# First block of a two-block transformer: the projection of queries, keys and values and the attention as one stage, head by head

## What is computed

```python
def project(h):
    q, k, v = jnp.split(h @ w_qkv, [A_WIDTH, 2 * A_WIDTH], axis=-1)
    q = rms_gain(q.reshape(B, -1, A_HEADS, 2, A_HEAD_DIM), q_gain)
    k = rms_gain(k.reshape(B, -1, A_HEADS, 2, A_HEAD_DIM), k_gain)
    return q, k, v.reshape(B, -1, A_HEADS, A_V_DIM)
q_l, k_l = apply_rope(q_l, rc, rs), apply_rope(k_l, rc, rs)   # latent tokens only
def attend(q, k, v):
    s = jnp.einsum('bqhcd,bkhcd->bhcqk', q, k).astype(jnp.float32) * scale
    p = jax.nn.softmax(s, axis=-1)
    a = (p[:, :, 0] - lam * p[:, :, 1]).astype(v.dtype)
    return jnp.einsum('bhqk,bkhe->bqhe', a, v)
def finish(o):
    o = rms_gain(o, subln_gain) * (1.0 - lam_init)
    return o.reshape(o.shape[0], o.shape[1], A_WIDTH) @ w_o
```

## Time and profile before

| | |
|---|---|
| median of three runs | 3884.35 us |
| the profiled execution, its time | 3887.47 us |
| its span in the profile | 3885.7 us |
| TensorE matmul busy | 3619.6 us, 93% of the span |
| TensorE weight load busy | 3133.7 us, 81% |
| VectorE, ScalarE, GpSimd busy | 2536.4, 1596.2 and 697.0 us |
| mean granted TensorE clock | 0.987 |

### The profile page before, as it was taken

One profiled execution on the slowest core, in us unless ns is written; L12 is line 12 of the kernel. 1 busy time (PEld: TensorE's weight loads), 2 busy tenths in 40 slices (PEclk: granted clock), 3 DMA queues, 4 the chain that ended last, 5 costly groups with the idle time before them and its releaser, 6 DMA issues.

```text
span 3885.7 us, 64997 instructions
## 1 busy us (share of the span) xinstructions
PE 3619.6 (93%) x25060; PEld 3133.7 (81%) x25060; DVE 2536.4 (65%) x5098; ACT 1596.2 (41%) x3541; POOL 697.0 (18%) x698
## 2 busy tenths in 40 slices
PE   8999999999999999999999999887889999988887
PEld 6888766788788876898778998777777798987776
DVE  4878547677755567655556776776554667676764
ACT  5222537322332235543235444444432454444443
POOL 0100002000000003000000244444400004444442
PEclk9999999999999999999999999999999999999999
DMA  6655211355434421554235799999942268999998
GB/s 257 203 187 188 87 55 44 114 184 183 159 114 141 141 99 39 196 184 164 78 109 196 318 420 421 420 421 420 420 160 110 89 240 359 420 421 420 420 420 340
DMA packets 134436, 909.40 MB, mean 234 GB/s; under 512 B 14823, under 2 KB 15079, under 8 KB 33264
## 3 DMA queue, kind: packets, MB, share of 16 engines
q0 software_dynamic: 93952, 615.72, 39.3%
q1 hardware_dynamic: 40176, 289.53, 20.5%
HBM read 904.11 MB, written 5.28 MB: 234 GB/s over the span
## 4 chain that ended last, share of the span: by engine, by line
PE 29%; DMA 15%; ACT 4%; DVE 3%; issue 1%; POOL 0%; DVEq 0%; ACTq 0%; POOLq 0%; PEldq 0%
PE ps L525 12%; PE ps L3030 11%; DMA arena<-peer_uv,arena 10%; DMA ada_t<-peer_uv,arena 5%; PE ps L757 5%; ACT L3093 1%; ACT L3060 1%; DVE arena L3237 1%; ACT arena L3097 1%; ACT arena L3094 0%; PE ps L2545 0%; POOL arena L3211 0%; DVE ada_t L3237 0%; ACT arena L3093 0%; ACT arena L3060 0%
## 5 line engine op out<-in xcount | busy, mean ns | idle before, releaser
L3030 PE MATMUL ps<-arena 128*128 128x128 f32 x6560 | 828.9, 282 | 139.7 <-ACT arena L3097 138.7
L3030 PEld LDWEIGHTS ps<-arena 128*128 128x128 f32 x6560 | 786.5, 195 | 189.2 <-ACT arena L3097 182.5
L3211 POOL DMA_INDIRECT arena<-peer_uv,arena x410 | 449.2, 1096 | 1329.5 <-DVEq L3172 770.3
L3237 DVE CUSTOM_DVE_ANT_0 arena<-arena 128x1024 f32<-128x1024 f32 x410 | 502.5, 1226 | 282.1 <-DMA arena<-peer_uv,arena 279.3
L722 DVE TENSOR_TENSOR w_lo<-wt,w_hi 128x1024 fp32r<-128x1024 f32 x389 | 476.5, 1225 | 305.2 <-ACT w_hi L704 280.1
L704 ACT ACTIVATE w_hi<-wt 128x1024 fp32r<-128x1024 f32 x389 | 408.8, 1061 | 587.0 <-PE ps L757 555.0
L757 PE MATMUL ps<-h_hi,w_hi 128*128 128x512 f32 (+1 forms) x1744 | 634.4, 366 | 8.6 <-ACT h_hi L950 3.5
L757 PE MATMUL ps<-h_hi,w_lo 128*128 128x512 f32 (+1 forms) x1744 | 626.7, 361 | 0.0
L757 PE MATMUL ps<-h_lo,w_hi 128*128 128x512 f32 (+1 forms) x1744 | 586.9, 361 | 1.0 <-DVE h_lo L970 1.0
L757 PEld LDWEIGHTS ps<-h_hi,w_hi 128*128 128x128 f32 x1744 | 330.3, 189 | 67.0 <-issue 11.8
L757 PEld LDWEIGHTS ps<-h_hi,w_lo 128*128 128x128 f32 x1744 | 330.5, 190 | 50.9 <-issue 1.1
(11 more groups left out here) (376 smaller groups left out, 5299.1 us busy)
## 6 DMA issues: line engine op xcount, KB each, us to landing
wt<-wstream SPq DMA_DIRECT2D x245, 1024.0 KB, 4.9
ada_t<-adastream POOLq DMA_DIRECT2D x128, 512.0 KB, 3.6
arena<-wstream SPq DMA_DIRECT2D x18, 1024.0 KB, 7.8
arena<-adafirst SPq DMA_DIRECT2D x8, 1024.0 KB, 15.6
arena<-peer_uv,arena POOLq DMA_INDIRECT x410, 19.4
arena<-bias_by_query POOLq DMA_DIRECT2D x2, 3072.0 KB, 14.6
bias_by_query<-bias_by_distance POOLq DMA_DIRECT2D x1, 4096.0 KB, 18.0
xT<-tokens SPq DMA_DIRECT2D x2, 1024.0 KB, 6.5
```

The source lines that it names most:

```text
L3030: ins = pe.matmul(y_banks(t)[m // 4][:, (m % 4) * P:(m % 4 + 1) * P], row[:, D + m * P:D + (m + 1) * P], diag[n % DIAGS], start=s == 0 and ...
L3211: pool.indirect_dma_start(out=rows[at % GB], out_offset=None, in_=peer_uv, in_offset=bass.IndirectOffsetOnAxis(ap=experts[:, t, s:s + 1], ...
L3237: dve.tensor_tensor_reduce(u, u, ztok[:, t], 1.0, 0.0, ALU.mult, ALU.add, hbuf[:, t, s:s + 1]).then_inc(dot_ready.sem, 1)
```

## The change

The 16 columns are ordered by head, query column and key column in turn (`A_COLS`), and the weight tiles with them. The first four columns (heads 0 and 1) and the values of heads 0 to 5 come first: columns 0 and 1, values of heads 0 to 3 (width 512), columns 2 and 3, values of heads 4 and 5 (width 256). Then a loop over the 32 units, now head by head, each head with its four blocks of queries (wide, wide, narrow, narrow). In steps 0 to 23 TensorE also projects columns 4 to 15, half a column in each step, in two pieces; their sum, root, norm, turn and sine are placed 2, 3, 4, 5 and 5 steps behind. The values of heads 6 and 7 (width 256) are made in steps 26 and 27. The transposed map and the output have one PSUM bank each; the turn of a column shares the output's bank; two banks go to the columns. There is no `end_phase` behind the projection. Roots of heads 0 and 1 are taken inside the stage. GpSimd's modulation loads wait for the last output to be stored, because two of the maps now lie in their buffer. In `values`, the sums of the two columns just made stand before chunks 1 and 2, their turns before chunks 4 and 5. The attentions of the later layers share one set of semaphores and count on from each other.

Within each step the order on the engines is: TensorE: scores, half of the column piece, transposes, turn, the other half, values, sum. ScalarE: square, root, copy of the transposed map, exponentials, weight split (odd steps), head work. VectorE: maximum, late values, norm, reciprocal, copy of the output, mix, sine, weight split (odd steps). Cut to its core:

```diff
+A_COLS = [at for h in range(A_HEADS) for at in (h * P, D + h * P)]
-        A_UNITS = [(h, q) for q in range(4) for h in range(A_HEADS)]
+        A_UNITS = [(h, q) for h in range(A_HEADS) for q in range(4)]
+        FIRST_COLS = 4
+        COLS_OVER = 2 * (N_COLS - FIRST_COLS)
+        LATE_AT = COLS_OVER + 2
+        turn_bank = ps[:, 4]
+        a_values = ps[:, 5, 0:P]
+        rot_bank = ps[:, 5, 0:LAT]
+        col_banks = [ps[:, 6], ps[:, 7]]
+        def column_at(i, behind):
+            c, odd = divmod(i - behind, 2)
+            return FIRST_COLS + c if not odd and 0 <= c < N_COLS - FIRST_COLS else None
+        def pe_a(pe, W, mm):
+            pe_by_chunk(pe, SW, [(A_COLS[c], both, col_banks[c]) for c in range(2)], TOK,
+                        lambda k, c: ("a_w_qkv", 0, k * P, c))
+            values(0, 0)
+            for c in (2, 3):
+                chunks(c, range(DC))
+            values(1, 2)
+            pe.wait_ge(D_.free, D_.claimed)
+            for i in range(n + LAG + 1):
+                if i < n:
+                    if q == 0:
+                        pe.wait_ge(QK.ready, 2 * (h + 1))
+                    if i >= 2:
+                        pe.wait_ge(SA.raised, i - 1)
...
+                if i < COLS_OVER:
+                    chunks(FIRST_COLS + i // 2, range(i % 2 * 4, i % 2 * 4 + 2))
+                if LAG <= i < n + LAG:
+                    pe.wait_ge(SA.even, u + 1)
+                    if u:
+                        pe.wait_ge(SA.kept, u)
...
+                if column_at(i, 5) is not None:
+                    pe.wait_ge(SA.stored, max(i - LAG - 1, 0))
+                    pe_col_rot(pe, mm, column_at(i, 5))
+                if i < COLS_OVER:
+                    chunks(FIRST_COLS + i // 2, range(i % 2 * 4 + 2, i % 2 * 4 + 4))
+                if i > LAG:
+                    pe.wait_ge(SA.kept, u + 1)
+                    if u:
+                        pe.wait_ge(SA.stored, u)
+                    pe.wait_ge(QK.read, rotated)
...
+                if column_at(i, 2) is not None:
+                    pe_col_sum(pe, mm, column_at(i, 2))
+                if i == LATE_AT:
+                    late(ws, (0, 1))
+                if i == LATE_AT + 1:
+                    late(ws, (2, 3))
+        def act_a(act, step):
+            for i in range(n + LAG):
+                if column_at(i, 2) is not None:
+                    act_col_squared(act, column_at(i, 2))
+                if column_at(i, 3) is not None:
+                    act_col_root(act, step, column_at(i, 3))
+                if i >= LAG:
+                    act.wait_ge(SA.turned, u + 1)
...
+                if i < n:
+                    act.wait_ge(SA.peaked, i + 1)
...
+                if i % 2:
+                    weights.ahead()
+        def dve_a(dve, step):
...
+                if i == LATE_AT + 2:
+                    late(1)
+                if column_at(i, 4) is not None:
+                    dve_col_normed(dve, step, column_at(i, 4))
...
+                if column_at(i, 5) is not None:
+                    dve_col_turned(dve, step, column_at(i, 5))
+                if i == LATE_AT + 1:
+                    late(0)
+                if i % 2:
+                    weights.ahead()
-        RUN_ON = (0, 2, 3, 4, 16, 24, 12, 13, 20, 21)
+        RUN_ON = (0, 1, 2, 3, 4, 16, 24, 12, 13, 20, 21)
```

More of the change, by code:

```diff
@@ new lines, in model_kernel, with __init__ @@
+        N_COLS = len(A_COLS)
+        FIRST_COLS = 4
+        class Columns:
+            def __init__(self):
+                self.projected, self.squared, self.summed, self.rooted, self.normed, self.rotated, self.read, self.ready = (
+                    sem(f"col_{k}") for k in
+                    ("projected", "squared", "summed", "rooted", "normed", "rotated", "read", "ready"))
+        QK = Columns()
+        raws, squares, roots = ([hT[:, 2 * n + i, :] for i in range(2)] for n in range(3))
@@ L1211, in pe_a_qkv @@
-            values(1, range(1, DC), banks)
-            pe_rot(pe, mm)
-            pe_rot(pe, mm)
-            SW.close()
-        def act_a_qkv(act, step):
-            weights = act_split_norm(act, A_QKV, 0, 1, TOK)
-            for i in range(A_COLS):
-                act_squared(act, step, TOK)
-                if i:
-                    act_root(act, step, TOK)
-                for _ in range(1 if i < A_COLS - 2 else 5 if i == A_COLS - 2 else 0):
-                    weights.ahead()
-            act_root(act, step, TOK)
-            weights.ahead()
+            both = ring_of_columns
@@ L1237, in values, with late @@
                     bank = D_.take()
-                    dve.tensor_copy(vA[:, t, half * 512:(half + 1) * 512], bank).then_inc(D_.free, 1)
-            last = A_COLS - 1
-            for i in range(last - 1):
-                weights.ahead()
-                dve_normed(dve, step, *A_OUTS[i], TOK)
-                if i:
-                    dve_turned(dve, step, A_OUTS[i - 1][0])
-            for _ in range(4):
-                weights.ahead()
-            values(0)
-            weights.ahead()
-            dve_turned(dve, step, A_OUTS[last - 2][0])
-            dve_normed(dve, step, *A_OUTS[last - 1], TOK)
-            dve_normed(dve, step, *A_OUTS[last], TOK)
-            weights.ahead()
-            values(1)
-            dve_turned(dve, step, A_OUTS[last - 1][0])
-            dve_turned(dve, step, A_OUTS[last][0])
-            assert not weights.left
+                    dve.tensor_copy(vA[:, t, half * 512:half * 512 + w], bank[:, 0:w]).then_inc(D_.free, 1)
+            def late(half):
+                dve.wait_ge(QK.projected, N_COLS + half + 1)
+                dve.tensor_copy(vA[:, 2 * half:2 * half + 2, 768:1024],
+                                col_banks[half].rearrange("p (t f) -> p t f", t=2)).then_inc(QK.read, 1)
             prod = tmp_b[:, 0:2 * HD]
@@ L1375, in dve_a_attend @@
-        def dve_a_attend(dve, step):
+            weights.ahead()
+            dve_col_turned(dve, step, 0)
+            dve_col_turned(dve, step, 1)
+            for _ in range(2):
+                weights.ahead()
+            values(0)
+            for _ in range(3):
+                weights.ahead()
+            for c in (2, 3):
+                dve_col_normed(dve, step, c)
+            weights.ahead()
+            for c in (2, 3):
+                dve_col_turned(dve, step, c)
+            values(1)
```

369 lines of the change are left out of this document (212 added, 157 removed).

## The result

The kernel before ran in 3883.98 us (median of 6 runs, 3882.87 to 3884.47), the changed kernel in 3895.64 us (6 runs, 3893.65 to 3900.62). The ratio is 1.003, interval 1.002 to 1.004: slower by 0.3%. The profiled execution of the changed kernel took 3893.89 us, 6.4 more than the profiled one of before (3887.47).

The account below looks back on a forecast made before the run. TensorE was taken to bound the stage, with 15.5 us to be had in its gaps; -16.7 + 1.2 + 1.7 + 0.7 + 7.7 + 13.5 = +8.1, plus 0.5 for the clock, gave 3893.0 us, range 3876 to 3903.

Parts of the forecast that it names:

- What goes: Gaps before first values and between projection and attention, first squares' wait, and 1.2 us at the output projection vanish: -16.7 us.
- the term of +1.2: Half the values, made in 192 matmuls of 256 columns instead of 96 wider ones, take 1.2 us more.
- Ahead of the steps: Before the attention steps: +1.2 for narrower value matmuls, +1.7 waiting for column 2's sine, +0.7 for value-bank copies; ends about 467.5.
- no gap over 2 us from the first column to step 23: Sign expected in the changed kernel's timeline: TensorE never idle over 2 us in that stretch.
- A head: In steps 0 to 23, 23.0 us per head instead of 21.4 of TensorE work; five times 1.6, taken as +7.7.
- lateness behind odd steps: Steps with columns: VectorE's next maximum starts 0.86 and 0.9 us late because the weight split ends after TensorE's scores.
- values in even steps wait for the copy: Sign in steps with columns: TensorE's values wait for the last output's copy from its single bank, 0.6 and 1.0 us.
- rival 1: TensorE stays the bound in steps with columns and the end loops are shorter: -4.6 us, 3879.7 us; chance 22 in 100.
- Steps 24 to 31: Without column pieces, each step is the loop scores, maximum, copy, values; TensorE's idle time there adds +13.5 us.
- The tail: About 11 us from unit 31 to first output matmul; head 1 follows head 0 by 3.7 us instead of 4.9, gaining 1.2.
- The clock: +0.5 us for one more short stretch at 1.2 GHz in steps 24 to 28, held for one case in four.
- rival 3: Clock falls in bare steps 24 to 31 and even-step waits before; four stretches, +17.3 us, 3901.7 us; chance 20 in 100.

Follow-up runs that it names:

- turn_before_split: The changed kernel with VectorE's sine of columns 2 and 3 ahead of the weight split in the stage's first part; ratio 1.0012 to the kernel before.
- split_first: The changed kernel with ScalarE's weight split at the start of odd steps instead of behind the exponentials; ratio 1.0024 to the kernel before.
- norm_behind: The changed kernel with VectorE's norm of a column behind the output's copy and the mix, not ahead of them; ratio 1.0015 to the kernel before.
- late_in_quarters: The changed kernel with the values of heads 6 and 7 in quarters in steps 24 to 27, not halves in 26 and 27; ratio 1.0006 to the kernel before.
- before_one_bank: The kernel before with one bank instead of two for its attention outputs; ratio 1.009 to the kernel before.
- all_five: The changed kernel with late values quartered, sine before split, split at odd steps' start, norm behind mix, outputs of units 25 and 27 in another bank; ratio 0.9982.
- changed_again: The changed kernel once more, without an edit, in a later session; ratio 1.0031 to the kernel before.
- clock_held: The changed kernel with five unused matmuls of 512 columns ahead of the turn in steps 24 to 26; ratio 1.0022 to the kernel before.

## Why the prediction was right

The direction was right, the time was forecast 2.6 us low (3893.0 against 3895.64, within the range of 3876 to 3903), and the trace's own difference, +8.3 in the stage, is close to the +8.1 of the sum before its 0.5 for the clock. That closeness hides errors that cancel.

- **What goes.** The gaps of 4.3 and 3.4 us are gone, the slow stretches behind them, and the wait for the first squares. Right. (For the matmuls of 256 columns the quotient 6.0 / 52 is 0.115, not 0.12; but in the traces they follow each other every 0.12 us, so the term of +1.2 stands.)
- **Ahead of the steps.** The waits were forecast at 1.7 and 0.7 and measured 2.2 (462.55) and 0.5 (the scores of unit 0). But behind the 2.2 us the clock fell, and a mean of 0.56 over 3.5 us is 3.5 x 0.44 = 1.5 us lost. With 0.5 more of wait that is the 2.0 us by which the scores of unit 0 started later than the forecast 467.5: they start at 469.53. I had looked for the fall of the clock in the attention steps and not here, where this wait was in the sum. turn_before_split, without wait and stretch, is 3.9 us shorter up to unit 0, where 2.2 + 1.5 = 3.7 were to be had by these rows, and split_first, with the wait and without the stretch, is 1.5 shorter. The sign "no gap over 2 us from the first column to step 23" failed by this wait.
- **A head.** Forecast 23.0 = 21.4 of TensorE's work and 1.6 of waits; measured 22.3, of which split_first and norm_behind, each of which removes waits in its own way, leave 21.9. The work was 0.5 us low and the waits came to 0.4, a quarter of what was forecast. The lateness behind odd steps was close: 0.82 and 0.57 against 0.86 and 0.9. What failed is the step from it to TensorE: TensorE's own step is longer than summed, so it comes to the bank later and meets the copy nearly done (copy's end 512.56, values 512.66). The extra 0.5 us is spread over the steps. In step 4, half of a column piece takes 1.49 us (487.12 to 488.61) where the sum has 1.36, because its first matmul lies 0.33 us ahead of the second instead of 0.23:

  ```profile
  487.12 0.50 PE L759 MATMUL ps<-h_hi,w_hi 128*128 128x512 f32 x1
  487.45 0.39 PE L759 MATMUL ps<-h_lo,w_hi 128*128 128x512 f32 x1
  ```

  There are eight such halves in a head; transposes and values are each a little shorter than summed and take back about half of it. So the sign "values in even steps wait for the copy" held for 0.2 us and less a step, not for 0.6 and 1.0. Over five heads this made 5 x 0.7 = 3.5 us less than forecast, and rival 1 is right on this point: in the steps with columns TensorE stays the bound.
- **Steps 24 to 31.** Scores of 24 to scores of 31 took 40.4 us. The forecast's idle times added to the work of each step by its rows make 6.3, 4.5, 9.7, 10.0, 4.45, 3.3 and 2.3, together 40.6; measured were 5.93, 4.65, 9.41, 10.18, 4.41, 3.40 and 2.42 us. The windows from 598.5 to 638.8 show 11.1 us without a busy PE instead of 13.5, since busy time there takes in the way of the last matmul through the array. Every term held within 0.4 us. late_in_quarters confirms the cause: cover for the same loops takes 6.4 of the 30.2 us away; before_one_bank confirms it from the other side, at 1.3 us per wide unit. In this the rule of the Trainium skill (Perfetto Trace Analysis, section Matmuls) on rotating banks is borne out as far as the forecast took it: a second bank matters where no independent work stands ahead of the reuse (all_five, 2.2 us from unit 28 to 31), and in the steps with columns it could have given no more than the 0.4 us per head that all waits cost there.
- **The tail.** 11.5 us from the last scores to the first output matmul, where about 11 was said. Head 1 came 5.4 us behind head 0, not 3.7, at a clock of 0.58 (window 650.3 to 655.7): the 1.2 us of gain that I had put there did not come, and instead the stretch behind the first output matmul is 1.2 us longer than before. The 3.7 itself was nearly right: in changed_again, at full clock there, head 1 comes 3.9 us behind (655.28 to 659.17). What had been left out is that the thin passage ahead of the first output matmul can lower the clock in the changed kernel as it does before.
- **The clock.** I gave it 0.5 us for one stretch in four cases. In the first profiled execution there was one, ahead of the steps, beside the one behind the first output matmul. In changed_again there were four windows below 1.00 in a row in the bare steps as well, for +5.1 us, and split_first had one behind the wait of step 24. So rival 3's mechanism acts in some executions and not in others. It may be why the six runs spread over 7 us where the six of before spread over 1.6, but that is not shown: in the later sessions the kernel before spreads by 7 to 9 us too. Nor does it explain by itself why the medians are 11.7 us apart and the stages of the traces 8.3: the profiled execution of before was 3.5 us above its median, that of the changed kernel 1.8 below. "It decides from the second stretch on, 3896" came near the median in the number. Its full size, four stretches and 3901.7, was not reached in the median. The rule that it went by, the Trainium skill, TensorE: Matmul & The Clock Gate, section A second HAM failure mode: psum-queue depth-cycling, is thus borne out in part: behind short waits between thin groups the clock fell in some executions (0.55 behind the wait of step 24 in split_first), and in others, with the same waits, it did not.

So the size of the forecast is right in part by luck: 2.0 us that I did not foresee at the start and 2.4 at the end (1.2 of loss for 1.2 of gain), against 3.5 forecast that did not come in the heads and some tenths elsewhere.

## What to carry to other kernels

When a stage's work is laid between another's, count for each step how much independent work the bound engine has before it wants the bank again; here one bank was all but enough with 1.4 to 2.7 us of other matmuls there, and cost the whole loop once these ran out, so spread the last filler over the steps where nothing else is left. In an engine that takes its program in order, put the operation for which the bound engine waits ahead of those for which it doesn't (here the sine ahead of a split). Compare stage lengths between marks that both traces have, since the busy times of the whole kernel show nothing of a change like this one.

## What was not expected of the hardware

- Behind much the same wait of TensorE the clock fell in one execution and not in another: with 0.71 us of work in 3.0 the window behind it is 1.00 in the first trace of the changed kernel, with 0.85 of 3.15 it is 0.61 in the second. Behind the 2.2 us wait at 462.55 it fell to 0.56, and behind the same wait in split_first it stayed at 1.00, a difference of 1.5 us. The other five traced executions with that wait all took the 1.5 us. In before_one_bank, with an idle time of 1.1 us at nearly every wide unit, it stood at 1.00 from 600 to 630 us, where TensorE was busy for 21.78 of 30 us.
- Five unused matmuls of 0.86 us where TensorE would wait cost nothing: the stage of clock_held is as long as that of the changed kernel's good trace. Its one traced execution shows 1.00 in these steps, and so does that good trace without them.
- The difference of one kernel between two sessions is larger than the effect: 3884 us against 3891 to 3894 for the kernel before. The sessions also differ in the chip, so which of the two makes the difference is open. Only runs of one session can be compared.
